# A router matmul turned round, with result-free matmuls in TensorE's waits

## The reference, cut to what matters

```python
h2 = rmsnorm(x, ffn_norm[layer])
# layer 1:
logits = jnp.einsum('bsd,de->bse', h, w_router)          # (256 x 1024) @ (1024 x 8)
top_v, top_i = lax.top_k(logits, 2)
top_w = jax.nn.softmax(top_v, axis=-1)
gate = jnp.sum(jax.nn.one_hot(top_i, 8) * top_w[..., None], axis=-2)
for e in range(8):
    y = y + gate[..., e:e + 1] * ((jax.nn.silu(h @ w1[e]) * (h @ w3[e])) @ w2[e])   # 1024 -> 3584 -> 1024
x = x + y
```

## Time and profile before

| what | value |
|---|---|
| median of 3 runs | 1592.75 us (1591.43 to 1595.17) |
| the profiled execution's own time | 1593.62 us |
| span of its profile | 1591.8 us (1.82 us of its time lie outside the span) |
| granted TensorE clock, mean | 0.989 |
| busy share PE, DVE, ACT | 97%, 80%, 66% |

### The profile page before, as it was taken

One profiled execution on the slowest core, in us unless ns is written; L12 is line 12 of the kernel. 1 busy time (PEld: TensorE's weight loads), 2 busy tenths in 40 slices (PEclk: granted clock), 3 DMA queues, 4 the chain that ended last, 5 costly groups with the idle time before them and its releaser, 6 DMA issues.

```text
span 1591.8 us, 23204 instructions
## 1 busy us (share of the span) xinstructions
PE 1549.4 (97%) x7253; PEld 1271.5 (80%) x7253; DVE 1267.9 (80%) x1329; ACT 1052.8 (66%) x1159; POOL 5.9 (0%) x12
## 2 busy tenths in 40 slices
PE   7999999999999899999999999999999999999997
PEld 6888888788888778878878878877887887887885
DVE  5885655446976679789789789789889979978978
ACT  6565544336564467677687687687778768767766
POOL 0000000000000000000000000000000000000000
PEclk9999999999999789999999999999999999999999
DMA  9444565358543679799899999999989989989985
GB/s 331 159 159 133 185 198 167 107 191 282 167 160 109 233 228 302 255 369 371 288 375 370 312 354 367 338 329 371 374 296 370 370 297 367 369 293 372 372 305 193
DMA packets 361372, 445.34 MB, mean 280 GB/s; under 512 B 17728, under 2 KB 272744, under 8 KB 361336
## 3 DMA queue, kind: packets, MB, share of 16 engines
q1 hardware_dynamic: 360768, 442.73, 82.1%
q0 software_dynamic: 480, 2.13, 0.4%
q10 hardware_dynamic: 88, 0.02, 0.0%
HBM read 443.76 MB, written 1.05 MB: 279 GB/s over the span
## 4 chain that ended last, share of the span: by engine, by line
PE 83%; DMA 4%; issue 4%; DVE 4%; ACT 3%; SPq 1%; DVEq 0%; ACTq 0%
PE bank L748 25%; PE bank L750 25%; PE bank L749 25%; DMA w_raw<-in_moe_w 4%; PE bank L1036 2%; ACT w_hi L450 2%; PE bank L1062 2%; DVE w_lo L1127 1%; SPq L351 1%; DVE hT_lo L1517 1%; PE bank L830 1%; PE bank L774 1%; ACT hT_hi L739 0%; DMA x_residual<-in_x 0%; PE bank L814 0%
## 5 line engine op out<-in xcount | busy, mean ns | idle before, releaser
L1127 DVE TENSOR_TENSOR w_lo<-w_raw,w_hi 128x1024 fp32r<-128x1024 f32 (+1 forms) x448 | 780.9, 1755 | 113.9 <-ACT w_hi L450 113.1
L450 ACT ACTIVATE w_hi<-w_raw 128x1024 fp32r<-128x1024 f32 (+1 forms) x448 | 663.9, 1492 | 160.2 <-PE bank L750 145.2
L748 PE MATMUL bank<-w_hi,hT_hi 128*128 128x512 f32 (+1 forms) x1424 | 568.4, 399 | 6.6 <-DVE hT_lo L1517 2.5
L750 PE MATMUL bank<-w_hi,hT_lo 128*128 128x512 f32 (+1 forms) x1424 | 555.6, 390 | 0.0
L749 PE MATMUL bank<-w_lo,hT_hi 128*128 128x512 f32 (+1 forms) x1424 | 554.4, 389 | 0.0
L748 PEld LDWEIGHTS bank<-w_hi,hT_hi 128*128 128x128 f32 x1424 | 269.3, 189 | 63.6 <-issue 6.7
L750 PEld LDWEIGHTS bank<-w_hi,hT_lo 128*128 128x128 f32 x1424 | 269.0, 189 | 56.7
L749 PEld LDWEIGHTS bank<-w_lo,hT_hi 128*128 128x128 f32 x1424 | 269.9, 190 | 50.8
L1122 DVE TENSOR_TENSOR w_lo<-w_raw,w_hi 128x2048 fp32r<-128x2048 f32 (+2 forms) x100 | 201.5, 2019 | 96.8 <-ACT w_hi L444 96.0
L444 ACT ACTIVATE w_hi<-w_raw 128x2048 fp32r<-128x2048 f32 (+2 forms) x100 | 169.6, 1699 | 161.1 <-PE bank L750 159.7
L748 PE MATMUL bank<-w_hi,hiddenM_hi 128*128 128x512 f32 x448 | 178.8, 399 | 1.1
(11 more groups left out here) (230 smaller groups left out, 1022.2 us busy)
## 6 DMA issues: line engine op xcount, KB each, us to landing
w_raw<-in_moe_w SPq DMA_DIRECT2D x448, 512.0 KB, 8.0
w_raw<-in_moe_w SPq DMA_DIRECT2D x448, 256.0 KB, 4.9
w_raw<-in_w_in SPq DMA_DIRECT2D x64, 512.0 KB, 4.6
w_raw<-in_dense_w SPq DMA_DIRECT2D x44, 512.0 KB, 4.8
w_raw<-in_dense_w SPq DMA_DIRECT2D x44, 256.0 KB, 2.8
w_raw<-in_w_out SPq DMA_DIRECT2D x16, 512.0 KB, 4.6
w_raw<-in_w_pool_proj SPq DMA_DIRECT2D x8, 512.0 KB, 4.5
w_raw<-in_w_attn_proj SPq DMA_DIRECT2D x8, 512.0 KB, 4.1
```

The lines of the kernel that those rows point to most:

```text
L450: act.activation(whi[:, m % SLOTS, 0:n], raw8[m % 8][:, 0:n], ACT.Copy).then_inc(s_hi, 1)
L748: pe.matmul(dst, ahi, bhi, start=start, stop=False)
L750: return pe.matmul(dst, alo, bhi, start=False, stop=stop)
L1127: dve.tensor_tensor(wlo[:, m % SLOTS, 0:n], raw8[m % 8][:, 0:n], whi[:, m % SLOTS, 0:n], ALU.subtract).then_inc(s_lo, 1)
```

## The change

The router matmuls are turned round: 8 router columns are stationary and 256 tokens move, so that there are 24 matmuls that give logits transposed (8x256) in one bank. DVE copies that to a new tile, PE transposes it back in two pieces, and DVE scales it as before. `norm(3)` on DVE moves behind the copy. ACT runs a Sqrt on a constant early, so that the table is loaded before it is needed. `x_rows_lo` is made for token tile 0 before the selection matrix and for tile 1 behind it, and the first gather takes the tokens tile by tile. Matmuls whose result nobody reads (`keep_busy`, 128x512) stand at four places: 4, 9, 3 and 6 of them. The two new tiles have sizes of 1024 and 64 bytes per partition.

```diff
+        lgT = sb("router_logitsT", [E, S])
+        sq0 = sb("sqrt_first", [P, 16])
...
                 hT_hi(3 * l + 2, 16 + 8 * l, (0, 1))
                 if l == 0:
                     ahead(c + 25)
+                else:
+                    act.activation(sq0[:, 0:1], cst[:, C_ONE:C_ONE + 1], ACT.Sqrt)
                 hT_hi(3 * l + 2, 16 + 8 * l, (2, 3))
                 norm(2 * l + 1)
...
+            def keep_busy(n, b):
+
+                for _ in range(n):
+                    pe.matmul(bank[b][:], aThi[:, 0, 0:P], aThi[:, 0:2, :], start=True, stop=True)
+
             layer(1, LAYER1, first=lambda: x_T(2, 1))
+            keep_busy(4, 5)
             x_T(3, 1)
...
                 for k in (2 * j, 2 * j + 1):
-                    for t in range(TT):
-                        ins = three(bank[4 + t][:, 0:E], hThi[:, k, t * P:t * P + P], hTlo[:, k, t * P:t * P + P],
-                                    wrhi[:, k, :], wrlo[:, k, :], k == 0, k == KC - 1)
+                    ins = three(bank[4][0:E, 0:S], wrhi[:, k, :], wrlo[:, k, :], hThi[:, k, :], hTlo[:, k, :],
+                                k == 0, k == KC - 1)
             ins.then_inc(s_rt, 1)
+            pe.wait_ge(s_lt, 1)
+            for t in range(TT):
+                ins = pe.transpose(bank[5][:, t * E:t * E + E], lgT[:, t * P:t * P + P], cst[0:E, C_ID:C_ID + E])
+            ins.then_inc(s_rl, 1)
+            keep_busy(9, 0)
             pe.wait_ge(s_mk, 1)
...
+            keep_busy(3, 0)
 
             def gather(i):
 
                 pe.wait_ge(s_sel, i + 1)
+                if isinstance(i, int):
+                    for t in range(TT):
+                        pe.wait_ge(s_xrl, t + 1)
+                        for j in range(2):
+                            for q in range(4):
+                                k = 4 * j + q
+                                for x in (xrhi, xrlo):
+                                    ins = pe.matmul(bank[2 + j][:, q * P:q * P + P], x[:, t, k * P:k * P + P],
+                                                    selR[:, t, :], start=(t == 0 and q == 0 and x is xrhi),
+                                                    stop=(t == TT - 1 and x is xrlo), skip_group_check=True)
+                            if t == TT - 1:
+                                ins.then_inc(s_g, 1)
+                    return
...
-            pe.wait_ge(s_xrl, 2)
             gather(0)
+            keep_busy(6, 0)
...
                 hT_lo(3 * l + 2, 16 + 8 * l, (2, 3))
-                norm(2 * l + 1)
+                if l == 0:
+                    norm(1)
...
             dve.wait_ge(s_rt, 1)
+            dve.tensor_copy(lgT[:], bank[4][0:E, 0:S]).then_inc(s_lt, 1)
+            norm(3)
+            dve.wait_ge(s_rl, 1)
             for t in range(TT):
-                ins = dve.tensor_scalar(lg[:, t, :], bank[4 + t][:, 0:E], st[:, 3, t:t + 1], None, ALU.mult)
+                ins = dve.tensor_scalar(lg[:, t, :], bank[5][:, t * E:t * E + E], st[:, 3, t:t + 1], None, ALU.mult)
...
-            for t in range(TT):
+
+            def rows_lo(t):
+
                 dve.wait_ge(s_xr, t + 1)
                 dve.scalar_tensor_tensor(xrlo[:, t, :], X[:, t, :], st[:, 3, t:t + 1], xrhi[:, t, :],
                                          ALU.mult, ALU.subtract).then_inc(s_xrl, 1)
 
+            rows_lo(0)
             dve.wait_ge(s_pos, 1)
...
             select(0)
+            rows_lo(1)
```

More of the change, by code:

```diff
@@ L256, in build @@
         s_rt = sem("router_done")
+        s_lt = sem("router_logitsT_in_sbuf")
+        s_rl = sem("router_logits_done")
         s_gd = sem("gate_diff")
```

## The result

The changed kernel takes 1612.3 us (median of 4 runs, 1609.7 to 1612.7) against 1592.5 us before: 19.8 us slower, ratio 1.012 with a 95% interval from 1.0107 to 1.0132. I had forecast 1587.0, 5.6 us faster. The profiled execution took 1612.65 us with a span of 1610.8.

The account below looks back on a forecast made before the run. PE was taken as the bound behind the router. An earlier first expert (4.4 us) and less half clock in the experts (1.2) sum to 5.6, off the median 1592.75: 1587.2, forecast as 1587, range 1582 to 1590.

Parts of the forecast that it names:

- Rival 3: Expert stage: weights from HBM set its pace and take the gain back, so the time is 1592.8; chance 0.07.
- Router matmuls: Router stage, PE: 24 matmuls of 256 columns at about 0.12 us, 2.9 us in sum; logits ready at about 540.05.
- The norm: Router stage, DVE: norm finished at 541.95, plus 0.25 us for POOL's clearing; scaling at 542.2 instead of 544.75.
- The conversion: Router stage, DVE instruction on 16 elements, 0.82 us before; now it comes when POOL is done and takes 0.2 us.
- Masks to gather: Router stage behind the scaling: counts 2.23 us later, one half of `x_rows_lo` ahead; gather at 546.9, a gain of 4.4 us.
- The result-free matmuls: Four, nine, three and six in PE's router-stage waits: free at full clock; at half the nine would cost 0.3 us.
- The clock: PE's clock between 542.9 and 546.9 decides the rest: fallen, the gain sums to 5.6 us; held, to 10.2 us.
- the forecast's likelier case: Clock falls between the nine matmuls and the gather, near 546: 5.6 us gained, 1587.2 us; chance 0.50.

## Why the prediction was wrong, by its steps

**The step that failed** is the one in the last sentence ahead of the rivals: "the chunk loads that start at 535.87 with x fill the raw slots as before". They did not. A chunk into one of the slots 4 to 7 took 3.01 us instead of 2.72, since the new tiles had moved these slots off a multiple of 256 bytes. With it fell "So behind the router PE is the bound, and a shift of its start should reach the end". In the loop PE takes 71.4 us for 25 chunks. Before, the transfers needed nearly as much: at the times from landing to landing above, 25 chunks are 71.0 us. With eight slow slots 25 x 3.01 = 75.3 stands against 74.8 measured: the transfers are the bound. A job takes 26.4 / 7 = 3.8 us more, some 3.4 of it there and some 0.4 in the rest. With the tiles last, where the slots are filled as before, the shift did reach the end: the jobs are as long as before and the gain of the router stage stays. I had read PE's waits and a DMA share of 1.09, and not the rate or the time from one landing to the next.

Behind it lies an omission. I counted what the change does in instructions and not what its two tiles do to the address of every tile behind them. The diff shows 1088 bytes ahead of `mixer` and `moe`; I costed them at nothing without naming them. Rival 3 named the expert stage, for another mechanism (the gain is swallowed, 1592.8), and could not give a loss. No rival held what happened.

**The router's steps**, from x's transposes, forecast, changed kernel, and before: logits ready 4.2, 4.2, 8.8; scaling 6.3, 7.5, 8.9; counts 8.5, 9.7, 11.7; gather 11.0, 13.0, 15.4; first expert 20.6, 22.4, 25.0.

- *Router matmuls*: right (537.40 - 537.29 = 0.11 apart).
- *The norm*: mechanism right, size off. DVE and POOL in the changed kernel:

```profile
538.06 1.55 DVE L1188 TENSOR_SCALAR norm_stats<-norm_stats 128x2 f32<-128x2 f32 x1
...
538.63 0.95 POOL L429 MEMSET hT_lo<- 128x1024 f32 x1
```

  An instruction on two elements took 1.55 us and ended at 539.61, 0.03 behind POOL's second clearing. In the kernel without result-free matmuls it took 0.66 and ended with the first clearing. In both it had begun 0.32 us behind POOL's first one, so its own start does not decide this; five of the seven profiles of kernels with the new router show 0.66 us and two show 1.55. What decides is open. I had allowed 0.25 us of delay, at most 0.5; it was 0.5 or 1.4. The Trainium skill, page SBUF — State Buffer, section Who interferes with whom, gives the exclusive lock of a port pair that I had weighed at one half. The trace agrees that the instruction is held while POOL clears (0.66 and 1.55 us instead of 0.17). The conversion fell to 0.17, as forecast.
- *Masks to gather*: counts 2.2 us behind the scaling, as forecast.
- *The result-free matmuls*: wrong for the three ahead of the gather. I costed them as free; at half clock they end at 546.68, and the gather stood behind them for about 0.8 us (the kernel without them starts it 0.5 us after the selection begins, this one 1.35).
- *The clock*: it fell, the forecast's likelier case, but at the counts and not behind them. It was back 1.5 us into the first expert; I had taken 3.3, by carrying over the 5.84 us of a single rise. In the first job this was worth 2.0 to 2.7 us and not 1.2, which gave back part of what the gather lost.

Together, in the kernel with the tiles last: 2.2 us in the router stage and 2.7 in the first job are 4.9, which is also what its median gained, against the 5.6 that I had summed. That the two come so close is in part luck: the gather begins 2.3 us later than forecast, for the norm and the three matmuls, and the clock's earlier return gives 1.5 us back. Nearly the whole miss of 25 us is the expert stage.

## What to carry to other kernels

A tile that is added in front moves every tile behind it: work out where the destinations of the large transfers land before costing anything else, and keep them at multiples of 256 bytes; small tiles go behind them. "PE is busy 97%" does not say that the transfers have room: compare the time from one chunk's landing to the next, slot by slot, with PE's time per chunk, and take two rates in one steady loop as a question. Matmuls without a result are free only up to the moment when the work behind them is ready, and at half clock they last twice as long (0.43 us from start to start instead of 0.22).

## What the runs showed of the hardware

- In long streams a row of 1 or 2 KB took 4.4 to 4.5 ns more on its DMA engine where its destination in SBUF started 128 bytes off a multiple of 256: 348 instead of 385 GB/s at 1 KB, 387 instead of 408 at 2 KB. Slots that start 64 bytes off had the same 348 GB/s in the expert stage. At 192 bytes only a short load was made, with a smaller loss (353 against 359). A source 128 bytes further on did not slow 1 KB rows.
- The 512-column matmuls of the second matrix started every 0.227 us where weights and the other operand had the same address modulo 256, every 0.229 with 64 bytes between, every 0.233 with 128.
- Whether the clock holds through the same instructions can differ from run to run. With 16 result-free matmuls the times of one kernel fell into two groups some 6 us apart, and the profiled executions of three such kernels show the gather twice at 1.00 and once at 0.50.
